# FFN 1 of a hybrid decoder step: gate and up as seven block products, all 22 pairs ahead of down

## What is computed

```python
def rmsnorm(x, g):
    y = x * lax.rsqrt(jnp.mean(x * x, axis=-1, keepdims=True) + NORM_EPS)
    return y * g

def swiglu(x, w_gate, w_up, w_down):
    return (jax.nn.silu(x @ w_gate) * (x @ w_up)) @ w_down

x = x + 0.5 * swiglu(rmsnorm(x, g_ffn1), ffn1_gate, ffn1_up, ffn1_down)
```

## Time and profile before

| | |
|---|---|
| time, median of 3 runs | 2459.64 us (2458.02 to 2460.93) |
| profiled execution, span | 2458.0 us (its own time is not listed apart; it equals the fastest run) |
| PE busy | 2413.0 us, 98% of the span |
| DVE, POOL, ACT busy | 1287.0, 1053.7, 579.2 us |
| matmuls | 21418 |

### The profile page before, as it was taken

The page is one execution under the profiler, slowest core; times in us unless marked ns, Lnnn a source line. Parts: engine busy times, 40 slices in busy tenths (PEclk is TensorE's granted clock), DMA queues, the critical chain, the costliest instruction groups (busy, mean ns, idle before and its releaser), DMA issues. The chain is left out here.

```text
span 2458.0 us, 50034 instructions
## 1 busy us (share of the span) xinstructions
PE 2413.0 (98%) x21418; PEld 2361.5 (96%) x21418; DVE 1287.0 (52%) x1843; ACT 579.2 (24%) x1084; POOL 1053.7 (43%) x604
## 2 busy tenths in 40 slices
PE   8999999999999999999998999999999999999998
PEld 8999999999999999999997888899999999999998
DVE  6851871671336255642466776666754444453225
ACT  4000010010011000010336676412433333341001
POOL 3434444344444344422340000244686868775550
PEclk9999999999999999999999999999999999999998
DMA  3111211111114432623451100062121212143211
GB/s 141 43 53 50 77 60 52 68 53 59 51 38 176 104 93 86 186 79 100 152 190 58 33 18 19 30 243 106 65 104 63 91 70 84 69 181 106 76 52 69
DMA packets 93733, 211.94 MB, mean 86 GB/s; under 512 B 16464, under 2 KB 42704, under 8 KB 92816
## 3 DMA queue, kind: packets, MB, share of 16 engines
q1 hardware_dynamic: 67184, 157.96, 19.2%
q10 hardware_dynamic: 26400, 51.82, 6.5%
HBM read 154.39 MB, written 54.20 MB: 85 GB/s over the span
## 5 line engine op out<-in xcount | busy, mean ns | idle before, releaser
L179 POOL TENSOR_TENSOR whi<-wraw,small 128x1024 fp32r<-128x1024 f32 (+3 forms) x134 | 227.9, 1701 | 844.9 <-PE ps L213 772.1
L213 PE MATMUL ps<-hhi,whi 128*128 128x344 f32 x1848 | 396.3, 323 | 0.0
L213 PE MATMUL ps<-hlo,whi 128*128 128x344 f32 x1848 | 392.9, 321 | 0.0
L213 PE MATMUL ps<-hhi,wlo 128*128 128x344 f32 x1848 | 391.5, 320 | 0.0
L182 POOL TENSOR_TENSOR wlo<-wraw,whi 128x1024 fp32r<-128x1024 f32 (+3 forms) x134 | 324.9, 2425 | 10.5
L213 PEld LDWEIGHTS ps<-hlo,whi 128*128 128x128 f32 x1848 | 313.4, 189 | 0.0
L213 PEld LDWEIGHTS ps<-hhi,whi 128*128 128x128 f32 x1848 | 311.1, 189 | 1.9 <-issue 0.7
L213 PEld LDWEIGHTS ps<-hhi,wlo 128*128 128x128 f32 x1848 | 309.5, 189 | 0.0
L3487 PE MATMUL ps<-t_hi,whi 128*128 128x258 f32 x704 | 143.7, 285 | 3.0 <-ACT ffn_gate L3394 1.0
L534 ACT ACTIVATE tmp<-tmp 128x1032 f32<-128x1032 f32 x22 | 23.5, 1068 | 504.2 <-DVE tmp L455 487.8
L3487 PE MATMUL ps<-t_lo,whi 128*128 128x258 f32 x704 | 142.2, 283 | 0.0
(11 more groups left out here) (513 smaller groups left out, 5056.8 us busy)
## 6 DMA issues: line engine op xcount, KB each, us to landing
wraw<-ffn_up SPq DMA_DIRECT2D x44, 512.0 KB, 3.2
wraw<-ffn_down SPq DMA_DIRECT2D x40, 384.0 KB, 3.0
wraw<-ffn_up SPq DMA_DIRECT2D x11, 1024.0 KB, 4.8
weights_raw_b<-ffn_up SPq DMA_DIRECT2D x11, 1024.0 KB, 4.7
a_spilled<-ffn_gate SPq DMA_DIRECT2D x18, 516.0 KB, 2.7
a_raw<-a_spilled SPq DMA_DIRECT2D x18, 516.0 KB, 4.4
wraw<-w_mix SPq DMA_DIRECT2D x18, 512.0 KB, 3.4
gates<-gate_out ACTq DMA_DIRECT2D x16, 516.0 KB, 2.8
```

What stands on the lines that cost most here:

```text
L179: pool.tensor_tensor(g.whi[:, s, 0:n], g.wraw[:, s, 0:n], g.zero.to_broadcast([P, n]), ALU.add).then_inc(g.w_hi, 1)
L213: last = pe.matmul(g.ps[:, 3 * bank_set + b, 0:BLK], w[:, s, k * P:(k + 1) * P], x(k, b), start=(k == 0 and first), stop=(k == kt - 1 and ...
```

## The change

`ffn_block` and its groups go; `first_ffn` takes their place. It runs FFN 2's scheme for all 22 pairs of FFN 1 and then all the down products in blocks of 6, 6, 6 and 4 tiles (`FIRST_BLOCKS`), every activation tile going through memory (22 in place of 0), and x being loaded a second time as the residual (`x_down`), 8 tiles. Pair 0 is made as eight plain products (`FIRST_PROD`), in which the four weight parts are used as they are, so that the first products need only even x tiles; pair 1 is the first with seven. The norm's squares are made by ACT from a second copy of x, rows of tokens (`x_rows`), 9 squares with a running sum, and PE no longer sums them. x itself is loaded as eight whole tiles, the odd ones on SP's queue behind both weight tiles, the even ones on ACT's queue. The set-up steps get a slot behind each pair from 2 to 20 with `PAIR_NS` = 5000 and one behind each down unit with `DOWN_NS` = 4000. The stores of x to memory become one per tile in the last down block, and two stores' waits ahead of the mixing layer go. In the later parts only semaphore counts move (offsets for what FFN 1 now adds to shared semaphores).

```diff
-FFN_GROUPS = (6, 6, 5, 5)
...
+FIRST_HI = [(n, q) for n in ("b11", "b21", "t1", "b22", "t2", "t3", "t4") for q in range(4)]
+FIRST_LO = FIRST_HI[:-4]
+HI0, LO0 = len(FIRST_HI), len(FIRST_LO)
+FIRST_PARTS = ((3, 0, 0), (0, 1, 0), (1, 0, 1), (2, 1, 1))
+FIRST_PROD = ((0, "b11", 2, True, None), (1, "b11", 0, True, None), (2, "b21", 4, True, None), (3, "b21", 6, True, None),
+              (0, "t1", 2, False, "p1"), (1, "t1", 0, False, "q1"), (2, "b22", 2, False, None), (3, "b22", 0, False, None))
+FIRST_BLOCKS = ((0, 6, (0, 1, 2, 3, 4, 5)), (6, 6, (6, 7, 10, 11, 16, 17)), (12, 6, (0, 1, 2, 3, 4, 5)),
+                (18, 4, (8, 9, 15, 16)))
+ROWS = -(-TOK // P)
+
+def first_ffn(nc, g, w_up, w_down, gcol, gnext, x_in, x_rows, consts_in, s5_in, a_dram, x_dram, setup, ahead, block):
...
+        sp.dma_start(g.wraw[:, 0, :], w_up[0]).then_inc(g.first_in, 16)
+        sp.dma_start(g.wraw[:, 1, :], w_up[1]).then_inc(g.st_in[0], 16)
+        for k in range(1, DT, 2):
+            sp.dma_start(g.x[:, k, :], x_in[:, k, :]).then_inc(g.x_in[k], 16)
+        load(0, 0, 1)
...
+        def one(i, b, j, between=None):
+            pair, n = 2 * b + j, 7 * j
+            a11, a12, a21, a22 = (part(j, r, c) for r in range(2) for c in range(2))
+            lo(i, b, n)
+            pool.wait_ge(g.st_in[j], i * 16 + 16 * (b + 1))
+            total("s1", sums(0), a21, a22, ALU.add)
+            g.fst_sum.wait(pool, i, pair, "s1")
+            total("s2", sums(1), sums(0), a11, ALU.subtract)
+            lo(i, b, n + 1)
+            total("s3", a21, a11, a21, ALU.subtract)
+            lo(i, b, n + 2)
+            lo(i, b, n + 3)
+            total("s4", sums(1), a12, sums(1), ALU.subtract)
+            lo(i, b, n + 4)
+            lo(i, b, n + 5)
+            if between:
+                between()
+            lo(i, b, n + 6)
...
+        for n, (s, r, c) in enumerate(FIRST_PARTS):
+            pool.wait_ge(g.st_hi, n + 1)
+            pool.tensor_tensor(place(g.wlo, s), part(0, r, c), place(g.whi, s).bitcast(F32), ALU.subtract)\
+                .then_inc(g.st_lo, 1 if n < 3 else 4)
+        for q in range(4):
+            pool.wait_ge(g.b_mixed, q + 1)
+            pool.tensor_scalar(g.x[:, 2 * q, late], g.x[:, 2 * q, late], gain(2 * q), None, ALU.mult).then_inc(g.b_scaled, 1)
...
+        for pair in range(2, NP):
+            j = pair % 2
+            G, U = halved(g.gate, j), halved(g.upv, j)
+            last = pair == NP - 1
+            done(v, 0, pair, 3)
+            g.fst_copy.wait(v, 0, pair, "p1")
+            on(v.tensor_tensor(G[0], two("y", j), G[0], ALU.add))
+            g.fst_up.wait(v, 0, pair, "g1a")
+            on(v.tensor_tensor(G[0], G[0], R[0], ALU.mult))
+            if last:
+                tile_low(0)
+            done(v, 0, pair, 4)
+            g.fst_copy.wait(v, 0, pair, "p5")
+            on(v.tensor_tensor(U[1], two("x", j), U[1], ALU.add))
+            g.fst_up.wait(v, 0, pair, "u2a")
+            on(v.tensor_tensor(U[1], U[1], R[1], ALU.mult))
+            if last:
+                tile_low(1)
+            done(v, 0, pair, 5)
+            g.fst_copy.wait(v, 0, pair, "u2")
+            on(v.tensor_tensor(G[1], two("z", j), G[1], ALU.add))
+            g.fst_up.wait(v, 0, pair, "g2a")
+            on(v.tensor_tensor(G[1], G[1], R[1], ALU.mult))
+            if last:
+                tile_low(2)
+            done(v, 0, pair, 6)
+            on(v.tensor_tensor(U[0], two("x", j), R[0], ALU.mult))
+            if last:
+                tile_low(3)
+            g.fst_up.wait(v, 0, pair, "u1")
+            g.fst_copy.wait(v, 0, pair, "silu1")
+            on(v.tensor_tensor(G[0], G[0], U[0], ALU.mult))
+            g.fst_copy.wait(v, 0, pair, "silu2")
+            on(v.tensor_tensor(G[1], G[1], U[1], ALU.mult))
+            if last:
+                tile_low(4)
+                tile_low(5)
+            else:
+                setup["vector"](pair, PAIR_NS)
+        for u in range(len(FIRST_BLOCKS) * DT):
+            b, k = divmod(u, DT)
+            xd = blocks(g.xd[:, k, :])
+            if u == 0:
+                v.wait_ge(g.x_in[0], 32)
+                v.wait_ge(g.m_half, 1)
+                v.scalar_tensor_tensor(xd, g.ps[:, 5:8, 0:BLK], 0.5, xd, ALU.mult, ALU.add).then_inc(g.set_free[1], 1)
...
+            setup["scalar"](act, pair)
+            hi(0)
+            if pair == 2:
+                full_silu(0, 1)
+            done(act, 0, pair, 0)
+            act.wait_ge(g.a_out[j], spilled[j] + 16 * (pair // 2))
+            on(act.activation(G[0], two("x", j), ACT.Copy))
+            hi(1)
+            if pair == 2:
+                full_silu(1, 2)
...
+        for n, (p, name, b0, start, copied) in enumerate(FIRST_PROD):
+            s = FIRST_PARTS[p][0]
+            pe.wait_ge(g.st_lo, p + 1 if p < 3 else 7)
+            if copied:
+                g.fst_copy.wait(pe, 0, 0, copied)
+            last = multiply(lambda k: place(g.whi, s, k), lambda k: place(g.wlo, s, k), name, b0, start, True)
+            if n != 2:
+                last.then_inc(g.st_done, 1)
...
+                else:
+                    g.fst_up.wait(pe, i, pair, "u2a")
+                pe.wait_ge(g.st_lo, i * 14 + (7 * pair + n + 1))
+                r = 7 * j + n
+                multiply(lambda k: ring(g.whi, r, k), lambda k: ring(g.wlo, r, k), name, bank(where, j), start,
+                         pair == 1).then_inc(g.st_done, 1)
+                if pair == 1 and n == 5:
+                    pe.wait_ge(g.rstd_small, 1)
+                    g.fst_up.wait(pe, 0, 0, "u1a")
+                    pe.wait_ge(g.c_in, 16 * 3)
+                    rate(range(8))
+                if pair == 1 and n == 6:
...
-SLOT_NS = 9000
+PAIR_NS, DOWN_NS = 5000, 4000
```

More of the change, by code:

```diff
@@ L839, in store, with scalar @@
            .then_inc(g.su_out[what], 16)
-    def scalar(act, turn):
-        while sent[0] < len(ready) and ready[sent[0]] < turn:
+    def scalar(act, slot):
+        while sent[0] < len(ready) and ready[sent[0]] < slot:
             store(act, sent[0])
@@ L2825 @@
 KEPT = 4
-A0, B0, X0 = FT, 2 * DT, 16
+A0, X0 = FT, 16 * DT
+BH0, BL0 = HI0 + DT, LO0 + DT
+M0, S0, T0 = 16, 4, 4
+DONE0, IN0, OUT0 = 7 * NP, 8 * NP, 8 * NP
+BACK0 = [16 * len(range(r, FT, 6)) for r in range(6)]
 SPILLED = NP - KEPT
@@ L2837, with __init__ @@
         ("b22", "z", False), ("t4", "x", False))
+SUMS, COPIES = ("s1", "s2", "s3", "s4"), ("p1", "p5", "u2", "silu1", "silu2")
+STEPS = ("g1a", "g1m", "u2a", "u2m", "g2a", "g2m", "u1", "a1", "a2")
 class Laps:
-    def __init__(self, sem, *names, first=()):
-        self.sem, self.names, self.first = sem, names, first
+    def __init__(self, sem, names, first=(), base=0):
+        self.sem, self.names, self.first, self.base = sem, names, first, base
     def value(self, i, pair, name):
@@ L2896, in plan_strassen @@
     g.st_in = [S("pair_in0"), S("pair_in1")]
-    g.st_sum = Laps(S("weight_sums"), "s1", "s2", "s3", "s4")
+    sums, copies, steps = S("weight_sums"), S("up_copies"), S("up_steps")
+    g.fst_sum = Laps(sums, SUMS)
+    g.fst_copy = Laps(copies, COPIES, first=[(0, n) for n in ("p1", "q1", "g2", "u2")] +
+                      [(1, n) for n in ("p1", "p5", "u2")] + [(0, "silu"), (2, "p1"), (1, "silu")])
+    g.fst_up = Laps(steps, STEPS, first=[("none", n) for n in range(6)] + [(0, n) for n in ("g1a", "u1a")] +
+                    [(1, n) for n in ("g1a", "u2a", "g2a", "u1")] + [(p, n) for p in range(2) for n in ("gm", "um", "a2")])
+    g.st_sum = Laps(sums, SUMS, base=NP * len(SUMS))
     g.st_hi, g.st_lo, g.st_done = S("part_hi"), S("part_lo"), S("part_done")
-    g.st_copy = Laps(S("up_copies"), "p1", "p5", "u2", "silu1", "silu2",
+    g.st_copy = Laps(copies, COPIES, base=NP * len(COPIES),
                      first=[(p, n) for p in range(2) for n in ("p1", "p5", "u2")] +
                      [(p, n) for p in range(2) for n in ("silu1", "silu2")])
-    g.st_up = Laps(S("up_steps"), "g1a", "g1m", "u2a", "u2m", "g2a", "g2m", "u1", "a1", "a2",
+    g.st_up = Laps(steps, STEPS, base=NP * len(STEPS),
                    first=[(0, n) for n in ("g1a", "u2a", "g2a", "u1", "g1m", "g2m", "u2m", "a1", "a2")])
@@ L2934, in low @@
         hi, lo = (b11, t1, b21, t2)[at]
[L2935 removed]
+        v.wait_ge(g.b_hi, BH0 + b_made(B_NAMES[at], pair))
         if scale is None:
```

878 lines of the change are left out of this document (561 added, 317 removed).

## The result

The change makes the kernel slower: 2507.02 us median (2506.59 to 2508.57, 4 runs) against 2460.28 (2458.02 to 2462.46, 4 runs), ratio 1.0192, 95% interval 1.0178 to 1.0207. The forecast was slower, with 2479 and a range from 2430 to 2502. The direction and most of the places were right, the size was not.

What follows compares the result with a forecast made beforehand. PE, busy 98%, was taken as the bound. Saving -48.8, slots +41, stores +7, start +13, seams +2 and clock +5 sum to +19.2 on the 2459.64 median: 2479 us, range 2430 to 2502.

Steps and rivals of the forecast that it cites:

- The bound and the saving: FFN 1: PE is the bound; seven products for eight save 2.44 us a pair over 20 pairs, -48.8 us.
- The slots and stores: Pairs of FFN 1: DVE set-up steps held back by POOL make PE wait, +41 us; stores waiting on ACT, +7.
- Stall 4.55 us: Pair behind a 28-step odd slot: t4, due at +17.54, waits for u2a until +22.1.
- 3.5 to 5.6 us for each: PE stall behind each of nine odd-pair slots, larger where a store waits at ACT too; +41 us in all.
- the three odd pairs' waits: Stores ahead of pairs 9, 15 and 17 delay the third product's copy: 2.9, 2.3 and 2.0 us, +7 together.
- The rival in which tensor-scalar steps escape: Slots: only steps reading two SBUF tensors are held; stall 1.8 us for 4.6, time 2468; no separate chance given.
- The start: Pairs 0 and 1: five waits, 19.9 us together, make some 74 us instead of 61, +13 us.
- 3.3 ahead of product 4: Start: product 4 waits for the low parts of t1 behind POOL, +3.3 us.
- 2.0 ahead of pair 1: Start: pair 1's first product waits for pair 0's last copy, +2.0 us.
- I take +5, two of the nine: Clock term: two of nine stalls followed by half clock, some 2.7 us each; bounds 0 and +24.
- Rival 3: Every stall behind the slots halves the clock: 2498 us, chance 0.12; sign, clock row at 0.50 in every even pair.
- Down and its seams: First down unit behind the last pair, and the last block with 4 tiles: +2 us.

Runs made afterwards that it cites:

- run 1: Changed kernel with set-up slots behind even pairs only, the odd pairs' steps moved behind the down units: 2459.85 us, ratio 1.0001 to the kernel before.
- run 3: Changed kernel with no set-up step behind any pair, all behind the first 22 down units at nominal 5600 ns: 2491.18 us, ratio 1.0129 to the kernel before.
- run 4: Changed kernel with ACT's stores in mid-pair and slots of 2400 instead of 5000 behind odd pairs: 2453.42 us, ratio 0.9974 to the kernel before.
- run 9: run 8 plus run 7's x loads, Newton rounds together, high parts 11 and 12 earlier, POOL's t4 low parts held for the factor's steps: 2436.48 us.
- run 10: Same as run 9 but without the hold on POOL's low parts of t4: 2437.71 us, ratio 0.9905 to the kernel before.
- run 2: Changed kernel with ACT's stores and their waits issued mid-pair, behind hi(5) and ahead of the silu: 2497.03 us, ratio 1.0153 to the kernel before.
- run 6: run 4 plus ACT's high part 11 ahead of four row squares and DVE's Newton rounds in one piece: 2453.98 us, ratio 0.9973 to the kernel before.
- run 5: run 2 plus 34 matmuls with unread results ahead of t4's wait in every even pair: 2479.97 us, ratio 1.0077 to the kernel before.
- run 7: run 4 plus x's even tiles loaded first, over both queues: 2450.57 us, ratio 0.9961 to the kernel before.
- run 8: run 2 with slots of 5600 behind even pairs, 1800 odd, 2600 down units, down's store behind the high part: 2437.17 us, ratio 0.9909 to the kernel before.

## Why the prediction was wrong

**The bound and the saving: right.** PE was the bound, an undisturbed pair takes 20.16 or 20.53 us (20.29 taken), and the 20 pairs save 47.5 for 48.8. The 0.37 by which even pairs are longer lies in their second and third products; its cause isn't shown.

**The slots and stores: the mechanism right, the sum in part by luck.** "Stall 4.55 us" in pair 4 was 4.22, the three odd pairs' waits were 3.09, 2.35 and 1.86 for 2.9, 2.3 and 2.0, and 48 us of pauses were 47.4. But "3.5 to 5.6 us for each" holds for five of the nine even pairs (4.1 to 4.7). In pairs 12, 14, 18 and 20, where a store waits too, the pause stood ahead of the third product and not of t4, and was 6.7, 2.9, 6.5 and 2.4 us; two too long and two too short made up the sum. Runs 1, 3 and 4 show that the steps behind odd pairs are the cause, runs 9 and 10 that POOL's operations hold them, run 2 that the stores cost what they were said to. The rival in which tensor-scalar steps escape is out too: in the slot ahead of pair 4 those at 122.67 and 126.46 took 1.27 and 1.22 us. By the Trainium skill, "SBUF — State Buffer", section "Who interferes with whom", such forms can take the ports shared with GpSimd; the trace agrees.

**The start: near in sum, by terms that made up for each other.** 14.6 for 13. Two of its waits, 3.52 ahead of t3 and 4.19 ahead of the factor's matmuls, were 4.3 (put one product later, ahead of b22) and 4.8 in the forecast. Those of 3.3 ahead of product 4 and 2.0 ahead of pair 1 were none and 0.56. In their place came the clock, which the forecast had not reckoned with at the start: t3 took 5.29 us for 2.87,

```profile
56.38:61.67 5.29, 5.29 (x24) 5.29 (x25) 0.81 (x5) 1.02 (x2) 4.19 (x4) 0.50 0.00 0
```

and the factor's 16 matmuls 3.49 for the 2.05 of run 9. Runs 6, 9 and 10 show that none goes alone: the next stands right behind it.

**The step that failed: "I take +5, two of the nine".** The clock cost some 18 us, 21.1 with what a pause leaves behind at full clock. The bounds, 0 and +24, held it; the choice between them was wrong, and so was its reason, that "PE is wholly idle only in one piece and at full work around it". No row said so. The rows showed one fall, behind 4.6 us in which PE had 121 small matmuls, and that was the only case near the new pauses. All nine stalls of the even pairs, and two of the three in odd pairs, were followed by a fall to 0.50. Run 5 prices it from the other side: with matmuls in the pauses the falls are gone, 18.1 us over nine pairs. Rival 3 (clock at every stall, 2498) had named the mechanism with a chance of 0.12, and its sign, 0.50 in every even pair, is what pairs 4 to 20 show; with the 9.5 us that the smaller terms below were over the forecast it comes to 2507.5, near the time measured, though by luck in part: it priced a stall at 2.7 us of clock, and run 5 makes it 2.0. Two numbers behind the bound were also loose. The row of 1.06 us is of three matmuls, not one, some 0.29 us each; and by the ratio given, 0.86 for 0.47, 6.8 us at half clock cost 3.1, not 2.7.

**What sets a fall isn't shown.** In pairs 2 to 21 of the changed kernel the pauses with a fall are all longer than those without, but a length alone doesn't decide. The first two rows are pair 20 in run 6 (run 7 has the same), the other two the wait ahead of t3 in run 2:

```profile
470.14:471.88 1.74, 0.00 (x1) 0.01 (x1) 1.67 (x4) 0.70 (x2) 0.00 (x0) 1.00 0.00 0
471.88:476.38 4.50, 4.50 (x24) 4.50 (x25) 2.34 (x3) 1.61 (x3) 3.85 (x3) 0.62 0.00 0
53.32:56.81 3.49, 0.00 (x2) 0.03 (x1) 3.46 (x7) 3.46 (x9) 1.38 (x1) 1.00 0.00 0
56.81:59.80 2.99, 2.99 (x24) 2.99 (x25) 0.82 (x5) 1.05 (x3) 1.86 (x2) 1.00 0.00 0
```

A pause of 1.74 us was answered and t4 took 4.50 us, one of 3.49 was not and t3 took 2.99; in run 3 one of 3.22 us in down wasn't either. So a stall of 1.7 to 3.5 us may cost its length or some 1.5 us more, and the runs don't show what decides.

**Smaller terms.** Down and its seams were mis-sized, 7.2 for 2. Some 4 of it came with a first down unit of 11.07 us behind a pause, and 3.4 from four units in which slots of 4000 and the activations' low parts together were more than DVE's 8.49 us; in run 8 these four are at 8.49. Behind FFN 1 4.3 us were lost that no term had. They come in steps of some 2 us or less between 1030 and 1600 us, and the other runs have 2 to 6 there. What causes them was not tried and stays open.

## What to carry to other kernels

When work is moved beside another engine, price its steps in the company they will have: a table that says 180 ns was right for DVE alone and too low by a factor of seven beside GpSimd. A stall of PE of a few microseconds has two prices, its length and the clock behind it, and the second is read from the trace; here moving the same steps by one pair took both away, but for two stores' waits. A new wait should be tested in the slot where the partner idles (behind even pairs) before the scheme that brought it is given up: with seven products and slots that fit, the kernel is 0.9% faster than before instead of 1.9% slower.

## What was not expected

- The clock's price: behind all eleven pauses of 2.35 to 6.72 us in pairs 2 to 21 the granted clock fell to 0.5 for some microseconds, and where no second pause lay among them the next 144 matmuls took 18.7 to 19.6 us for 17.4. Behind those of 1.65 and 1.86 it did not, but in runs 6 and 7 it did behind one of 1.74, and in run 2 not behind one of 3.49. 34 matmuls in each of ten pairs, whose results nobody reads, made the kernel 17 us faster.
- Twelve DVE steps on 9 columns took 2.4 us with GpSimd held and 13.1 beside it.
- At the start of the kernel the first matmuls of the run with x's even tiles first ran at 0.21 us each up to 15.3 us, with a clock column of 1.00 that has no entry behind it. The first matmuls before did the same: three of 344 columns took 0.86 us until 11.6. So an earlier x was worth 3 us, not 4.
